# Long and short matmuls of a k-tile, grouped by bank instead of by length

## The reference: what is computed

```python
u = h @ w_in_even[e]                       # 2048 x 6144
x = x + jnp.concatenate([y_a, y_b], axis=-1) @ w_out_even[e]
u = h @ w_in_odd[o]                        # 2048 x 8192
x = x + (att * jax.nn.silu(gate)) @ w_out_odd[o]
q = (h @ wq); k, v = jnp.split(m @ wkv, 2, axis=-1)   # per layer, 256 memory rows
return o @ wo                              # per layer
```

## Time and profile before

| | |
|---|---|
| median of three runs | 1662.64 us |
| the profiled execution's own time | 1663.41 us |
| its span, from the first to the last instruction | 1661.5 us |
| mean granted TensorE clock | 0.998 of full |
| PE busy | 1644.6 us (99%), 9688 matmuls |
| PEld busy | 1438.1 us (87%) |
| DVE, ACT, POOL busy | 1144.9, 789.9, 182.8 us |
| DMA | 296.50 MB, mean 178 GB/s |

### The profile page before, as it was taken

The page is one execution under the profiler, slowest core; times in us unless marked ns, Lnnn a source line. Parts: engine busy times, 40 slices in busy tenths (PEclk is TensorE's granted clock), DMA queues, the critical chain, the costliest instruction groups (busy, mean ns, idle before and its releaser), DMA issues.

```text
span 1661.5 us, 26699 instructions
## 1 busy us (share of the span) xinstructions
PE 1644.6 (99%) x9688; PEld 1438.1 (87%) x9688; DVE 1144.9 (69%) x1241; ACT 789.9 (48%) x932; POOL 182.8 (11%) x126
## 2 busy tenths in 40 slices
PE   9999999999999999999999999999999999999998
PEld 7888888888888888888888888888888888888887
DVE  7856697777776766667765567767666776766554
ACT  6633434465554444445433345555555554444332
POOL 0000060000004310043100000000000013400143
PEclk9999999999999999999999999999999999999999
DMA  9666755555555554457666665556556556554453
GB/s 307 200 189 184 230 177 172 178 171 159 165 175 177 186 169 140 144 168 231 185 185 193 188 188 176 167 164 188 166 183 181 176 165 194 186 163 141 129 189 113
DMA packets 291059, 296.50 MB, mean 178 GB/s; under 512 B 9024, under 2 KB 288704, under 8 KB 291008
## 3 DMA queue, kind: packets, MB, share of 16 engines
q1 hardware_dynamic: 290864, 295.73, 58.1%
q10 hardware_dynamic: 144, 0.07, 0.0%
HBM read 293.68 MB, written 2.10 MB: 178 GB/s over the span
## 4 chain that ended last, share of the span: by engine, by line
PE 97%; DVE 1%; DMA 1%; ACT 0%; issue 0%; DVEq 0%; ACTq 0%
PE ps L255 60%; PE ps L258 30%; PE ps L309 2%; PE ps L327 1%; DVE wpair L775 0%; PE ps L453 0%; PE ps L468 0%; PE ps L367 0%; DMA raw<-xa_wkv 0%; PE ps L460 0%; DMA par<-params 0%; PE ps L318 0%; PE ps L390 0%; PE ps L422 0%; PE ps L417 0%
## 5 line engine op out<-in xcount | busy, mean ns | idle before, releaser
L775 DVE TENSOR_TENSOR wpair<-raw,wpair 128x1024 fp32r<-128x1024 f32 x544 | 699.1, 1295 | 313.0 <-ACT wpair L519 310.2
L519 ACT ACTIVATE wpair<-raw 128x1024 fp32r<-128x1024 f32 x544 | 575.3, 1059 | 713.3 <-PE ps L258 705.7
L255 PE MATMUL ps<-xpair,wpair 128*128 128x512 f32 x1920 | 608.3, 398 | 0.0
L255 PE MATMUL ps<-ypair,wpair 128*128 128x512 f32 x1536 | 483.8, 396 | 6.9 <-DVE ypair L862 3.0
L258 PEld LDWEIGHTS ps<-xpair,wpair 128*128 128x128 f32 x1920 | 360.6, 188 | 85.2
L258 PE MATMUL ps<-xpair,wpair 128*128 128x256 f32 x1920 | 377.8, 278 | 0.0
L258 PEld LDWEIGHTS ps<-ypair,wpair 128*128 128x128 f32 x1536 | 288.5, 188 | 68.2
L258 PE MATMUL ps<-ypair,wpair 128*128 128x256 f32 x1536 | 301.9, 278 | 0.0
L255 PEld LDWEIGHTS ps<-xpair,wpair 128*128 128x128 f32 x1920 | 293.6, 189 | 1.7 <-issue 0.6
L255 PEld LDWEIGHTS ps<-ypair,wpair 128*128 128x128 f32 x1536 | 234.0, 189 | 8.3 <-issue 8.1
L255 PE MATMUL ps<-wpair,ypair 128*128 128x512 f32 x512 | 160.8, 395 | 0.0
(11 more groups left out here) (176 smaller groups left out, 908.7 us busy)
## 6 DMA issues: line engine op xcount, KB each, us to landing
raw<-xa_wkv SPq DMA_DIRECT2D x128, 512.0 KB, 4.1
raw<-w_in_odd SPq DMA_DIRECT2D x128, 512.0 KB, 3.9
raw<-w_in_even SPq DMA_DIRECT2D x96, 512.0 KB, 3.7
raw<-xa_wq SPq DMA_DIRECT2D x64, 512.0 KB, 3.5
raw<-xa_wo SPq DMA_DIRECT2D x64, 512.0 KB, 3.4
raw<-w_out_even SPq DMA_DIRECT2D x32, 512.0 KB, 3.7
raw<-w_out_odd SPq DMA_DIRECT2D x32, 512.0 KB, 4.3
xkT<-mem SPq DMA_DIRECT2D x8, 512.0 KB, 7.2
```

The costliest lines, as they stand in the source:

```text
L255: mm(ps[:, 2 * parity + j, :], still[:, k, 0, j * P:(j + 1) * P], move[:, k].rearrange("p h n -> p (h n)"), start=(k == 0), stop=False)
L519: fn(wpair[:, KP * p:KP * (p + 1), 0, :], raw[:, p], ACT.Copy).then_inc(hi_ready, 1)
L775: v.tensor_tensor(wpair[:, kp, 1, :], raw[:, p], wpair[:, kp, 0, :].bitcast(F32), ALU.subtract).then_inc(lo_ready, 1)
```

## The change

The second of two loops over `j` is dropped, so that the short matmul stands in the loop of the long one. Before, a k-tile is long into bank 0, long into bank 1, short into bank 0, short into bank 1 (banks of the even parity). Now it is long and short into bank 0, then long and short into bank 1. The matmuls, their operands, their flags, and the waits and increments are the same; the short matmul's line is now 257.

```diff
                     for j in range(2):
                         mm(ps[:, 2 * parity + j, :], still[:, k, 0, j * P:(j + 1) * P],
                            move[:, k].rearrange("p h n -> p (h n)"), start=(k == 0), stop=False)
-                    for j in range(2):
                         last = mm(ps[:, 2 * parity + j, S:2 * S], still[:, k, 1, j * P:(j + 1) * P], move[:, k, 0],
                                   start=False, stop=(k == KT - 1))
```

## The result

The changed kernel takes 1676.55 us, the median of four runs (1672.6 to 1676.98), against 1662.65 us before (1662.48 to 1663.17). The ratio is 1.0078, with a 95% interval of 1.0064 to 1.0092: slower by 0.8%, some 14 us. Its times are also spread over 4.4 us, where those of before are within 0.7 us. The profiled execution is the quickest of the four, 1672.6 us; its span is 1670.8 us, 9.3 us more than before. Of the executions reported further down, one of the nine of e6 took 3312.46 us, twice as long as the other eight, at an unchanged clock; nothing here explains it, and it is left out.

A forecast was written before the change was run, and what follows sets the result against it. The prediction took PE's matmul pace to bound the kernel: 1515 us of k-tiles + 146 us of the rest + 0 for the change = 1661.5 us of span, forecast 1663 us, no change, range 1648 to 1683 us.

The forecast's parts named there:

- The likeliest case: Whole kernel: no change that can be told (under 0.2%), 1663 us, itself 1660 to 1666; chance 0.50.
- its upper part: Slower side of the range, mostly 1667 to 1683 us: same bank, or steps costing a little more than their columns; 0.29.
- What bounds the kernel.: Whole kernel: PE's matmul pace bounds it, PE busy 1644.6 of 1661.5 us, its waits only 9.4 us.
- Long and short matmuls have the same price per column, so what sets the pace goes with the columns streamed.: Matmuls of a k-tile: 0.453 ns a column for both lengths, 0.696 us a k-tile.
- the term for the neighbours by length: Within a k-tile: changing which length follows which costs 0, with some room on both sides.
- If a step costs what the matmul ahead of it streams, the sum is the same.: Four steps of a k-tile: 0.464 + 0.232 = 0.696 us in both orders.
- The bank.: Short matmul adding to the bank the long one just wrote: taken at 0, usual end 19.6 us, far end 59 us.
- the same bank costs: Rival: short matmul waits for the bank the long one still writes, 19.6 us, 1682 us; case chance 0.29.
- the mark of the bank: Sign in the changed kernel's trace: a chunk longer by 0.14 us if the same bank costs.
- The crowded loads: Rival: weight loads under neighbouring short matmuls cost now; spreading gains 7 ns a k-tile, 15 us, or up to 30 us; 0.21.

The follow-up runs named there:

- e6: Changed kernel, but the first k-tile of each piece (one in four) ordered as before, two long then two short: 1666.82 us without the one long execution.
- e3: Kernel before the change, its order kept, but all four matmuls of a k-tile sent to bank 0 (nearly throughout a chunk): 1662.62 us.
- e1: Kernel before, but from a chunk's second k-tile on long and short of bank 0, then short and long of bank 1: 1664.16 us.
- e5: Changed kernel, but the first k-tile of each chunk ordered as before, two long then two short: 1668.05 us, ratio 1.0033 to the kernel before.
- e8: Kernel before with the two short matmuls of each k-tile dropped, only the long ones kept: 1369.28 us, one execution.
- e10: Kernel before, but behind a chunk's first k-tile each long matmul is replaced by a second short one: 1384.8 us, one execution.

## Why the prediction was right and wrong

The measured time lies in the range of 1648 to 1683 us. The likeliest case, no change at 1663 us, was not what happened; slower had a chance of 0.29. That the range held was partly luck: its upper part was priced by a cost of the bank that isn't there.

*What bounds the kernel.* Right: PE's pace alone. The waits went from 9.4 to 9.7 us, and no other engine came in.

*"Long and short matmuls have the same price per column, so what sets the pace goes with the columns streamed."* **This step failed**, and with it the term for the neighbours by length, taken at 0, which came out at 9 to 14 us. The numbers under it were right (0.464 and 0.232 us), the inference wasn't. Long ones alone take 0.2267 us and short ones 0.120 us, 0.443 and 0.469 ns a column. That both came out at 0.453 ns in the order of before was a coincidence: in that order the long pair takes 0.464 us, where two long ones alone take 0.453 us, and the short pair 0.232 us, where two short ones alone take 0.240 us. The trace held the warning: the 0.1205 us of line 327, which the prediction set aside, are just the price of a short matmul.

*"If a step costs what the matmul ahead of it streams, the sum is the same."* Failed for the same reason, in a form that the prediction hadn't: it is no small difference between kinds of step, but a rhythm that lasts for a whole stretch and has two values.

*The bank.* Taken at 0, and rightly: e3 shows 0.01 us, within the noise, for four neighbours in one bank, and this with the fp32r matmuls, for which the prediction had rows of other forms only. The rival "the same bank costs" gave the right sign and nearly the size, 1682 us, by the wrong mechanism. Its sign would have fitted too: a chunk in the slow pace is 0.16 us longer than before, and the prediction had set 0.14 us as the mark of the bank. Only e1 to e3 tell the two apart. The chance that slower was given rested mostly on it. The Trainium skill's advice to use all banks for parallelism ("Perfetto Trace Analysis", section "Matmul Optimizations") showed no effect on matmuls that follow one another here: e3 has nearly all of them in half as many banks and takes the same time.

*The crowded loads.* Not found as described: in the fast stretches of the changed kernel the two short steps of a k-tile take 0.230 us together, against 0.232 us before, some 2 ns less where the rival had 7 ns or more. The part of it that held is that 56 ns of a k-tile are something other than columns: by the streams of one length 53.3 ns go with the four matmuls, 13.3 ns each, and the 3.3 ns left go with the order. Only the 3.3 ns can be won by another order. The Trainium skill gives the columns over 2.4 GHz and 2.5 ns for the isolated gap of a warm matmul, and says that in a stream of weight loads and matmuls both set the spacing ("TensorE: Matmul & The Clock Gate", section "Back-to-back issue gap"). The form agrees with these runs, but the constant of these fp32r matmuls with a weight load each is 13.3 ns.

**What stays open** is what keeps the rhythm and why it has two values. That PE's own order of matmuls drives it is shown by the flips of e5 and e6, at the k-tiles that were regrouped; that it lives in PE, and not in the memories that PE reads and writes, is likely but not shown. Nor was it tested whether the 13.3 ns belong to the weight load or to the fp32r form. What picks it at a restart isn't settled: neither the kind of break nor the order of the first k-tile does so alone.

## What to carry to other kernels

Where PE never waits, the order of matmuls of different lengths is worth measuring by itself, and a mean price per column read from one order can't be carried to another. Take the price of each length from a stretch of that length alone. Their sum was the floor in every trace here, and what the present order has above it was all that reordering could win (3.3 of 697 ns). A pattern with one stable pace is worth more than one that is sometimes faster, and a spread that grows from 0.7 to 4 us between runs can be a sign of several paces.

## What the runs showed of the hardware

- fp32r matmuls with a weight load of 128 columns each, one kind at a time and at the 2.4 GHz level of the clock: 0.2267 us for 512 columns and 0.120 us for 256 (e8, e10).
- Alternating in length, the same matmuls run at 0.693 or 0.707 us a k-tile. The pace is kept through whole stretches, 190 us where nothing breaks them, and a single k-tile in another order changes it (91 of 102 times in e5). Two thirds of the profiled execution's k-tiles are slow.
- Neighbouring matmuls in one bank cost nothing against neighbours in two (e3, 1662.62 against 1662.61 us with 2176 k-tiles).
